# Six of eight up blocks of a feed-forward from seven products of quarters, and the neighbouring conditioning tiles moved in pairs

## What is computed

```
def modulate(x, g, shift, scale):
    return rmsnorm(x, g) * (1.0 + scale[:, None, :]) + shift[:, None, :]

mod = silu(c) @ w_ada[l] + b_ada[l]          # six vectors of 1024 for each layer l
h = modulate(x, g_mlp[l], shift, scale)      # 512 x 1024
x = x + gate * (square(relu(h @ w_ff1[l])) @ w_ff2[l])      # w_ff1 1024 x 4096, w_ff2 4096 x 1024
```

## Time and profile before

| | |
|---|---|
| median of three runs | 2262.08 us (2260.95 to 2263.88) |
| span of the profiled execution | 2260.0 us |
| first feed-forward in it | about 267 to 637 us |
| second feed-forward in it | about 811 to 1161 us |
| TensorE busy | 2187.5 us, 97% |
| VectorE busy | 1422.1 us, 63% |
| ScalarE busy | 964.7 us, 43% |

### The profile page before, as it was taken

One profiled execution on the slowest core, in us unless ns is written; L12 is line 12 of the kernel. 1 busy time (PEld: TensorE's weight loads), 2 busy tenths in 40 slices (PEclk: granted clock), 3 DMA queues, 4 the chain that ended last, 5 costly groups with the idle time before them and its releaser, 6 DMA issues.

```text
span 2260.0 us, 31907 instructions
## 1 busy us (share of the span) xinstructions
PE 2187.5 (97%) x13243; PEld 1930.6 (85%) x13243; DVE 1422.1 (63%) x2141; ACT 964.7 (43%) x1460; POOL 177.9 (8%) x155
## 2 busy tenths in 40 slices
PE   6999999999999999999999999999999999999998
PEld 3877988888898898899898999987778889889997
DVE  5777565655577667565556667754665445676674
ACT  3656342313256645454444334434444324334442
POOL 7310000000032100000020000002002001000000
PEclk8999999999999999999999999999999999999999
DMA  6442255555521122332421332323112331233230
GB/s 236 149 147 94 94 168 186 186 181 192 183 86 57 39 67 83 112 106 81 141 65 66 122 94 93 113 84 111 52 47 87 114 112 57 82 105 113 95 111 38
DMA packets 127749, 245.70 MB, mean 109 GB/s; under 512 B 4779, under 2 KB 36870, under 8 KB 127478
## 3 DMA queue, kind: packets, MB, share of 16 engines
q1 hardware_dynamic: 122848, 228.02, 29.9%
q0 software_dynamic: 4096, 15.28, 2.0%
q10 hardware_dynamic: 662, 0.37, 0.1%
HBM read 241.56 MB, written 2.10 MB: 108 GB/s over the span
## 4 chain that ended last, share of the span: by engine, by line
PE 83%; DVE 9%; ACT 3%; DMA 3%; issue 2%; POOL 0%; SPq 0%; DVEq 0%; ACTq 0%
PE PS L66 82%; DVE t L75 5%; ACT t L72 3%; DVE t L83 2%; DMA t<-in_ffn_w_dram 1%; DVE t L86 1%; PE PS L69 1%; DMA t<-in_w_ada_dram 1%; DVE t L79 1%; DVE t L92 0%; DMA t<-in_w_ff_dram 0%; DVE t L80 0%; POOL t L75 0%; SPq L101 0%; DVE t L95 0%
## 5 line engine op out<-in xcount | busy, mean ns | idle before, releaser
L66 PE MATMUL PS<-t,t 128*128 128x256 f32 (+4 forms) x12876 | 2137.9, 329 | 40.8 <-issue 9.2
L66 PEld LDWEIGHTS PS<-t,t 128*128 128x128 f32 (+2 forms) x12876 | 1886.2, 189 | 288.4 <-issue 53.1
L72 ACT ACTIVATE t<-t 128x1024 fp32r<-128x1024 f32 (+7 forms) x738 | 654.3, 903 | 938.0 <-DVE t L75 463.5
L75 DVE TENSOR_TENSOR t<-t,t 128x1024 fp32r<-128x1024 f32 (+9 forms) x693 | 778.4, 1140 | 378.1 <-ACT t L72 330.3
L72 ACT ACTIVATE t<-PS 128x512 f32<-128x512 f32 (+4 forms) x331 | 177.2, 549 | 224.6 <-PE PS L66 169.8
L75 DVE TENSOR_TENSOR t<-t,PS 128x512 f32<-128x512 f32 (+2 forms) x134 | 83.2, 625 | 145.4 <-PE PS L66 139.2
L75 POOL TENSOR_TENSOR t<-t,t 128x512 f32<-128x512 f32 (+2 forms) x71 | 85.0, 1198 | 1093.8 <-ACT t L72 934.3
L72 ACT ACTIVATE t<-t,t 128x256 fp32r<-128x256 f32 (+5 forms) x220 | 115.9, 535 | 96.4 <-DVE t L83 45.4
L83 DVE SCALAR_TENSOR_TENSOR t<-t,t,t 128x1024 f32<-128x1024 f32 (+2 forms) x157 | 144.0, 924 | 16.3 <-DMA t<-in_w_ada_dram 10.8
L83 DVE SCALAR_TENSOR_TENSOR t<-PS,t,t 128x512 f32<-128x512 f32 (+3 forms) x128 | 82.1, 649 | 87.6 <-PE PS L66 82.1
L69 PE MATMUL PS<-t,t 128*128 128x128 f32 (+1 forms) x367 | 59.2, 302 | 27.9 <-DVE t L79 8.0
(11 more groups left out here) (30 smaller groups left out, 154.3 us busy)
## 6 DMA issues: line engine op xcount, KB each, us to landing
t<-in_w_ff_dram SPq DMA_DIRECT2D x64, 1024.0 KB, 5.3
t<-in_ffn_w_dram SPq DMA_DIRECT2D x60, 1024.0 KB, 5.0
t<-in_w_ada_dram SPq DMA_DIRECT2D x36, 1024.0 KB, 6.1
t<-in_w_ada_dram POOLq DMA_DIRECT2D x24, 512.0 KB, 4.3
t<-in_w_in_dram SPq DMA_DIRECT2D x12, 1024.0 KB, 5.0
t<-in_swa_w_qkv_dram SPq DMA_DIRECT2D x6, 1024.0 KB, 5.8
t<-in_ffn_w_dram SPq DMA_DIRECT2D x8, 768.0 KB, 4.4
t<-in_w_in_dram SPq DMA_DIRECT2D x24, 256.0 KB, 3.6
```

Of the source, the lines that this page charges most:

```text
L66: return Instr(self.real and self.real.matmul(o, lhs, rhs, start=start, stop=stop, **more))
L72: return Instr(self.real and self.real.activation(o, src, func, **more))
L75: return Instr(self.real and self.real.tensor_tensor(o, a, b, op))
```

## The change

The first feed-forward takes the form of the second, with the same functions, which now get the layer as a number. So six of its up blocks, of 96 matmuls of 512 columns, become units of 168 matmuls of 256 columns, and there are five rounds in place of four. One of the three t buffers for the sums of h (TH0) lies elsewhere for this stage, because the accumulator t25 is in use. h is kept in float32 where the hidden buffers were.

The 28 tiles of w_ada don't stand behind one weight each any more. Two stand ahead of the third up weight, two ahead of the fourth, and then two ahead of each of the twelve down weights of the first four rounds; none stands between the weights of units. So a vector's four tiles stand ahead of two weights in a row. The columns of a vector are one weight later in MOD_AT where the weight ahead of `after` is an ordinary one, and VectorE now does every tile up to the weight `after` ahead of its addition.

```diff
+        def ff0_plan():
+            w1, w2 = wt(A["w_ff1"][0]), wt(A["w_ff2"][0])
+            vecs = [(0, v, u) if v == 5 and not late else (1, v, u)
+                    for late, v in ((0, 5), (1, 1), (1, 0), (1, 2), (1, 4), (1, 3), (1, 5)) for u in range(4)]
...
+            for t, n in enumerate((0, 0, 2, 2)):
+                c, k = t // 2, 4 * (t % 2)
+                ada_next(n)
+                weight("up0", w1[:, k:k + 4, 512 * c:512 * c + 512], 4, 512)
+            for q, chunks in enumerate(FDOWNS):
+                for c in FUNITS[q]:
+                    unit("s3", w1, 512 * c)
+                for n in range(2):
+                    for c in chunks:
+                        ada_next(2)
+                        weight("down0", w2[:, 4 * c:4 * c + 4, 512 * n:512 * n + 512], 4, 512)
...
                 after = next(x[1] for x in PLAN[p:] if x[0] == "w")
                 if after >= WX["mo"][2]:
-                    MOD_AT.setdefault(after - 2, []).append(it[1:3])
+                    MOD_W[it[1:3]] = after
+                    MOD_AT.setdefault(after - (2 if WT[after - 1]["m"] is None else 1), []).append(it[1:3])
...
         def dve_step(e, w, split=True):
             for l, v in MOD_AT.get(w - 1, ()):
+                dve_split(e, MOD_W[l, v])
                 dve_columns(e, l, v)
...
-        def pe_ff1(e, nm, nxt):
-            pe_up1(e, 0, nm)
-            pe_up1(e, 1, nm)
+        def pe_ff(e, l, nm, nxt):
+            pe_up(e, l, 0, nm)
+            pe_up(e, l, 1, nm)
             for q in range(5):
                 for c in FUNITS[q]:
-                    pe_unit(e, 0, c, 0, nm)
+                    pe_unit(e, FF[l], c, 0, nm)
...
-            pe_ff1(e, n_ff1, n_glu1)
+            pe_ff(e, 1, n_ff1, n_glu1)
```

More of the change, by code:

```diff
@@ L376, in bass_two_blocks, with ada_next @@
         square("mo", w_mo)
[L378 to L397, removed]
+        FUNITS, FDOWNS = ((), (2, 3), (4, 5), (6, 7), ()), ((0,), (1, 2), (3, 4), (5,), (6, 7))
+        def ff0_plan():
+            w1, w2 = wt(A["w_ff1"][0]), wt(A["w_ff2"][0])
+            vecs = [(0, v, u) if v == 5 and not late else (1, v, u)
+                    for late, v in ((0, 5), (1, 1), (1, 0), (1, 2), (1, 4), (1, 3), (1, 5)) for u in range(4)]
+            def ada_next(n):
+                for _ in range(min(n, len(vecs))):
+                    l, v, u = vecs.pop(0)
+                    ada(l, v, us=(u,))
+            for t, n in enumerate((0, 0, 2, 2)):
[9 more added lines that the diff above has]
+                        weight("down0", w2[:, 4 * c:4 * c + 4, 512 * n:512 * n + 512], 4, 512)
+            assert not vecs
+        ff0_plan()
         for n in (0, 2, 1):
@@ L1864, in dve_hidden @@
[L1864 to L1892, removed]
-                        s = ta.take(key, (hid_lo, key))
-                        e.wait_ge(acc, key)
-                        e.wait_for(ta.free(key))
-                        e.activation(TMP[s][:, COLS[hf]], PS[:, banks[key], COLS[hf]], ACT.Relu).then_inc(relu, key)
-                        act_hidden(e, q % 2, k, hf, key)
@@ L1916, in pe_up_keys @@
-        def pe_up_keys(l, q):
-            for n2 in range(2):
-                for n in range(4):
-                    for h in range(2):
-                        hid_at[q % 2, 4 * n2 + n, h] = (("up", l, q, n2), n, h if q == 0 and n2 == 0 else F)
[L1922 to L1926, removed]
-                pe_up_keys(l, q)
-                for n2 in range(2):
-                    last = q == 3 and n2 == 1
-                    pe_linear(e, (("down", l, q), n2), down_ws(l, q, n2), FOUR, hid_of(q % 2),
-                              x_until(("down", l, q), 4 * n2), halves=last, mid=pe_close(e, nxt) if last else None)
@@ L2556, in act_unit @@
             act_keep(e, u, 2, 2, "x", Q12)
-            if i and (c, gate) == (2, 0):
+            if i not in LAYER and (c, gate) == (2, 0):
                 act_t_hi(e, i, 4)
@@ L2618, in dve_unit @@
             dve_low(e, u, Q22)
-            if i:
+            if i not in LAYER:
                 dve_low(e, u, Q11)
@@ L2789, in act_ff1 @@
                 for n2 in range(2):
[L2790 to L2791 removed]
+                    act_resid(e, ("down", l, q), nxt if q == 4 else None, 4 * n2, f_ws(l, q, n2),
+                              halves=q == 4 and n2 == 1, weighted=l == 1)
                     if q == 0:
[L2793 to L2796 removed]
+                        act_t_hi(e, FF[l], 3 + n2)
```

188 lines of the change are left out of this document (73 added, 115 removed).

## The result

| | before | after |
|---|---|---|
| median | 2261.51 us (2260.64 to 2263.88) | 2318.81 us (2317.25 to 2322.87) |
| span of the profiled execution | 2260.0 us | 2317.9 us |
| TensorE busy | 2187.5 us | 2196.1 us |
| VectorE busy | 1422.1 us | 1483.7 us |

What follows compares the result with a forecast made beforehand. TensorE, busy for 97% of the span, was taken as the bound. -9.7 + 3.2 + 9.2 + 3.7 + 37.8 + 8.8 = +53.0 us, on 2260.0 plus 2.1, gave 2315.1 us, range 2297 to 2330.

Steps and rivals of the forecast that it cites:

- The units: First feed-forward: six blocks of 21.85 us become units of 20.23 us, saving 9.7 us.
- The third up weight: Start of the first feed-forward: two tiles ahead of this weight on VectorE lengthen TensorE's existing wait by 3.2 us.
- The first vector's columns: After the first half block, TensorE's bias product waits for all four tiles of the first vector: 9.2 us.
- The first pair: First pair of units: 1.7 us more as in the second feed-forward, plus 2 for VectorE's four tiles: 3.7 us.
- The three changes: From units to down blocks: TensorE's columns wait for the vector's last two tiles, 12.6 us three times, 37.8 in all.
- The clock: Behind each of four long waits TensorE restarts at half clock and loses 2.2 us, 8.8 in all.
- At nothing: Costed at zero: h in fp32, one t half in TMP, the later sliding-window norm, SyncE's queue of loads.
- the opening: Start of the first feed-forward: waits of 3.2 us at the third up weight and 9.2 at the first vector's columns.

Runs made afterwards that it cites:

- e3: The changed kernel without the 28 w_ada tiles of the first feed-forward, columns kept, so seven vectors are wrong: 2253.56 us, 0.9972 of the kernel before.
- e1: The changed kernel with each vector's columns one weight later, ahead of the weight behind its last tile: 2296.46 us.
- e6: The changed kernel with columns one weight later for only five of the seven vectors, not in the two rounds with one chunk: 2300.52 us.
- e9: The changed kernel without the tiles of the three vectors whose columns stand between a pair of units and its first down block: 2281.96 us.
- e10: The changed kernel without the four tiles of the first vector, columns kept, so this vector is wrong: 2312.61 us.
- e4: The kernel before, all blocks linear, no units, with the w_ada tiles in pairs as in the changed kernel: 2300.64 us, 1.0174 of the kernel before.
- e8: The changed kernel with unread matmuls filling TensorE's idle time ahead of four columns, rerun beside the unchanged changed kernel: 2314.31 us against 2319.19.

## Why the prediction was right

The total was off by 3.7 us, and the range held it. Step by step:

- **The units**, 9.7 saved: e3 shows 7.6 by the medians (4 to 9 by the ratio), with some 1 us of waits in the first pair in it, and TensorE busy for 2175.9 us, 11.6 under before. Right within the noise.
- **The third up weight**, +3.2: the wait in the earlier trace rows of 1.42 is 4.44, +3.0. Right.
- **The first vector's columns**, 9.2: measured 7.28. VectorE was on time by the working: 12.4 us from the first square (288.21) to the last low half, then 5.3 of tiles. TensorE was late: its 60 matmuls took 9.33 us and not 7.2, because after the wait of 4.44 it ran at half clock. The two terms were summed as if they stood apart; TensorE's lost clock came out of its next wait.
- **The first pair**, 3.7: measured 0.58 + 0.18. The 2 us that VectorE's four tiles were to add did not come, probably because the long wait ahead (7.28) had put VectorE ahead of TensorE again; no run tests that alone. And the 1.7 from the template was read too high: it is the difference of two windows, and in the longer one only 0.85 is idle time.
- **The three changes**, 12.6 each: 12.86 each. The template's own times and the position of each instruction were enough. VectorE's rows (first tile 394.02, low half 398.72, join 401.52, last low quarter 406.03, last two tiles 406.64) follow the working within 0.3 us.
- **The clock**, 2.2 at each of four waits, 8.8: measured 18.3 to 18.5, with a fifth place behind the 4.44. This is the term that was mis-sized. The earlier trace rows has a restart at which 5.5 us ran at half clock, and one with 3.4, a loss of 2.7 and 1.7; the prediction took 2.2, with 3.4 as the upper bound, for which no row was given. Here 7 to 10 us ran at half clock behind each of the four, a loss of 3.5 to 4.8, over the upper bound too. The Trainium skill, "TensorE: Matmul & The Clock Gate", section "HAM oscillation — how this bites in real kernels", tells of a kernel in which each group of matmuls behind a wait starts cold and pays the transition again; the traces agree for the waits of 2.9 us and more, while of five waits of 1.97 in e1 and e6 only two were followed by half clock (1.7 lost).
- **At nothing**: nothing new waits elsewhere in the stage of the changed kernel. But e9 and e10 show that this was so because the long waits hid it: what was costed at nothing would have been 3.8 to 5.1 us at three places, with its clock. The prediction counted VectorE's work in the down blocks (some 20 of 43.7 us) and found it small enough; it did not ask which bank the columns there need, and behind what it is emptied.

So the sum held partly by luck: the clock was 9.6 too small, the first pair and the opening 5.0 too large. The side and the main mechanism didn't depend on that; 38.6 of the 57.9 are in the step in which the working put them.

## What to carry to other kernels

Where a kernel already has a stage of the new form, its rows give the durations, and the order of instructions gives the places; the end of each chain can then be computed to 0.3 us. Ask of every wait on TensorE what else is late behind it: removing some of several waits gave back a third (e10) to three quarters (e9) of their cost. Ask too which bank an instruction takes, and what empties it: columns at the opening of a block waited 3 to 4 us for a bank though their tiles were done. And place side work by what stands behind it in all three orders, that of the engine, that of the loads and that of the engine which copies the loaded weight; one tile behind each weight, with columns in the middle of blocks, costs no wait, where two in a row with columns at the opening of blocks cost 39 us.

## What the runs showed of the hardware

The half-clock stretch behind a wait did not grow with the wait. Summed over windows of up to 15 us behind each wait of this stage, it cost 3.3 to 4.8 us behind 12.86 us, 2.2 to 4.5 behind 6.9 to 9.8, 3.0 to 4.8 behind 3.6 to 4.1, but only 1.6 to 2.7 behind the 4.4 to 4.7 at the opening (eight traces), 4.4 behind the 5.11 of e10, behind 2.93 still 1.7 (the window 403.40 to 418.40 of e4 has a clock of 0.89), and behind 1.97 nothing or 1.7. In e8 a filled place with only 0.40 us of idle time ahead of it lost 1.7 twice, and once nothing. So with TensorE at full clock before it, a wait of 2.9 to 4.7 us cost 1.4 to 2.3 times its length, and the wait alone does not say which.
